# The low halves of three gate slabs on GpSimd instead of VectorE, in a two-layer hybrid decoder trunk

## The reference

```python
proj = jnp.einsum('bsd,dn->bsn', h, w_in)
cq, ckv, kr, qkv_b, qkv_c, iq, ik, iw, gate_logits = split_columns(proj)
# the indexer of C: 16 heads
dots = jnp.einsum('bqhd,bsd->bqhs', iqi, ik)
score = jnp.einsum('bqhs,bqh->bqs', jax.nn.relu(dots), iwi) * idx_scale
# the gates: 3 x 1024 columns of w_in
g_a, g_b, g_c = jnp.split(jax.nn.sigmoid(gate_logits), 3, axis=-1)
merged = g_a * y_a + g_b * y_b + g_c * y_c
x = x + g1 * (merged @ w_out)
```

## Time and profile before

| | us |
|---|---|
| median of 3 runs | 975.89 |
| the runs | 975.89, 978.88, 974.9 |
| the profiled execution's own time | 971.84 |
| its span, first to last instruction | 969.6 |
| TensorE busy | 913.4 |
| VectorE busy | 708.9 |
| ScalarE busy | 499.6 |
| GpSimd busy | 29.4 |

### The profile page before, as it was taken

One profiled execution on the slowest core, in us unless ns is written; L12 is line 12 of the kernel. 1 busy time (PEld: TensorE's weight loads), 2 busy tenths in 40 slices (PEclk: granted clock), 3 DMA queues, 4 the chain that ended last, 5 costly groups with the idle time before them and its releaser, 6 DMA issues.

```text
span 969.6 us, 12842 instructions
## 1 busy us (share of the span) xinstructions
PE 913.4 (94%) x5020; PEld 779.2 (80%) x5020; DVE 708.9 (73%) x1145; ACT 499.6 (52%) x738; POOL 29.4 (3%) x53
## 2 busy tenths in 40 slices
PE   8998979998997999999989998899989889999998
PEld 5887969976975788888868997898679668888886
DVE  5987889787787667585675788988878856565454
ACT  6455775455447343443573478374453754343441
POOL 1010000000000000000010000000000000000000
PEclk9999999999999999999999999999999999999999
DMA  9978723414652757775466884251445345645441
GB/s 377 410 305 365 249 88 131 174 44 174 261 204 100 272 208 272 285 280 202 150 241 210 303 320 155 88 205 56 173 170 223 138 150 196 244 152 205 173 174 44
DMA packets 29581, 198.12 MB, mean 204 GB/s; under 512 B 3281, under 2 KB 3793, under 8 KB 7506
## 3 DMA queue, kind: packets, MB, share of 16 engines
q1 hardware_dynamic: 23474, 155.22, 42.8%
q0 software_dynamic: 5760, 41.95, 11.5%
q10 hardware_dynamic: 288, 0.14, 0.1%
HBM read 196.24 MB, written 1.05 MB: 203 GB/s over the span
## 4 chain that ended last, share of the span: by engine, by line
PE 55%; DVE 28%; ACT 8%; issue 5%; DMA 3%; DVEq 0%; ACTq 0%
PE bank L566 13%; PE bank L567 13%; PE bank L568 13%; DVE w_lo L1315 9%; PE bank L527 3%; PE bank L529 3%; PE bank L528 3%; ACT w_hi L965 3%; DMA raw<-in_slabs_dram 3%; DVE front L1322 3%; DVE acc L1622 2%; DVE score L1531 2%; DVE score L1549 1%; PE bank L902 1%; DVE acc L1322 1%
## 5 line engine op out<-in xcount | busy, mean ns | idle before, releaser
L1315 DVE TENSOR_TENSOR w_lo<-raw,w_hi 128x2048 fp32r<-128x2048 f32 (+2 forms) x146 | 316.3, 2172 | 111.2 <-ACT w_hi L965 109.2
L965 ACT ACTIVATE w_hi<-raw 128x2048 fp32r<-128x2048 f32 (+2 forms) x146 | 262.8, 1806 | 96.5 <-PE bank L568 65.1
L566 PE MATMUL bank<-w_hi,h_hi 128*128 128x512 f32 x536 | 214.1, 400 | 10.4 <-DVE w_lo L1315 7.3
L567 PE MATMUL bank<-w_hi,h_lo 128*128 128x512 f32 x536 | 210.6, 393 | 0.0
L568 PE MATMUL bank<-w_lo,h_hi 128*128 128x512 f32 x536 | 210.4, 393 | 0.0
L566 PEld LDWEIGHTS bank<-w_hi,h_hi 128*128 128x128 f32 x536 | 101.5, 189 | 36.1 <-issue 7.9
L568 PEld LDWEIGHTS bank<-w_lo,h_hi 128*128 128x128 f32 x536 | 101.5, 189 | 22.1
L567 PEld LDWEIGHTS bank<-w_hi,h_lo 128*128 128x128 f32 x536 | 101.4, 189 | 19.9
L527 PE MATMUL bank<-h_hi,w_hi 128*128 128x256 f32 x384 | 111.5, 290 | 5.7 <-DVE w_lo L1315 5.7
L528 PE MATMUL bank<-h_lo,w_hi 128*128 128x256 f32 x384 | 108.6, 283 | 0.0
L529 PE MATMUL bank<-h_hi,w_lo 128*128 128x256 f32 x384 | 108.6, 283 | 0.0
(11 more groups left out here) (206 smaller groups left out, 1399.9 us busy)
## 6 DMA issues: line engine op xcount, KB each, us to landing
raw<-in_slabs_dram SPq DMA_DIRECT2D x124, 1024.0 KB, 4.8
front<-in_ada_dram POOLq DMA_DIRECT2D x31, 1024.0 KB, 5.7
acc<-in_ada_dram POOLq DMA_DIRECT2D x9, 1024.0 KB, 8.1
raw<-in_slabs_dram SPq DMA_DIRECT2D x16, 552.0 KB, 5.0
front<-in_ada_dram SPq DMA_DIRECT2D x5, 1024.0 KB, 10.7
raw<-in_slabs_dram SPq DMA_DIRECT2D x6, 768.0 KB, 5.9
proj<-in_ada_dram SPq DMA_DIRECT2D x2, 1024.0 KB, 8.6
x_t<-in_x_dram SPq DMA_DIRECT2D x2, 512.0 KB, 4.4
```

Of the source, the lines that this page charges most:

```text
L566: nc.tensor.matmul(o, hh, wh, start=first, stop=False)
L567: nc.tensor.matmul(o, hl, wh, start=False, stop=False)
L965: nc.scalar.activation(w_hi[:, n % RING, 0:w], raw[:, n % RING, 0:w], ACT.Copy).then_inc(hi_ready.sem, 1)
L1315: nc.vector.tensor_tensor(w_lo[:, n % RING, 0:w], raw[:, n % RING, 0:w], w_hi[:, n % RING, 0:w], ALU.subtract).then_inc(lo_ready.sem, 1)
```

## The change

GpSimd makes the low halves of the slabs `S_GATE1`, `S_GATE1 + 1` and `S_GATE1 + 2` in both layers, behind its ten loads and before `spread_gate`, and counts them on a semaphore of its own, `lo_pool`. VectorE no longer makes them. Whoever waits for a low half (SyncE before it reloads a place, TensorE before it multiplies) asks `split(l, s)`, which gives the semaphore and the count for this slab.

```diff
+POOL_LO = [S_GATE1 + g for g in range(3)]
@@
-        lo_ready = event("lo_ready", NS)
+        lo_ready = event("lo_ready", NS - len(POOL_LO))
+        lo_pool = event("lo_pool", len(POOL_LO))
@@
+        def split(l, s):
+
+            if s in POOL_LO:
+                return lo_pool.sem, lo_pool.at(l, POOL_LO.index(s) + 1)
+            return lo_ready.sem, lo_ready.at(l, s + 1 - sum(p < s for p in POOL_LO))
@@ SyncE, load
                 if n >= RING:
-                    sp.wait_ge(lo_ready.sem, n - RING + 1)
+                    sp.wait_ge(*split(*divmod(n - RING, NS)))
@@ GpSimd
                 for _ in range(10):
                     load_ada(n)
                     n += 1
+                for s in POOL_LO:
+                    m = l * NS + s
+                    pool.wait_ge(hi_ready.sem, m + 1)
+                    nc.gpsimd.tensor_tensor(w_lo[:, m % RING, :], raw[:, m % RING, :], w_hi[:, m % RING, :], ALU.subtract)\
+                        .then_inc(lo_pool.sem, 1)
 
                 pool.wait_ge(idx_sc.sem, idx_sc.at(l, IDX_HEADS))
@@ TensorE
             def slab(l, s):
-                pe.wait_ge(lo_ready.sem, lo_ready.at(l, s + 1))
+                pe.wait_ge(*split(l, s))
@@ VectorE, in the loop over the indexer's heads
                     if h == 7:
                         pair_norm(1, C_B, ss16b, 2 * A_QK, K_FAC)
-                        lo(l, S_GATE1)
-                    if h == 11:
-                        lo(l, S_GATE1 + 1)
@@ VectorE, after it
                 k_rows(0)
                 k_rows(1)
-                lo(l, S_GATE1 + 2)
```

## The result

The changed kernel takes 980.09 us (median of 17 runs), the kernel before 973.63 us over as many: 1.0061 times as long, 95% interval 1.0047 to 1.0075, so 4.6 to 7.3 us more (the two medians alone lie 6.5 us apart). Forecast were 6.4 us more and 982.3 us. The 2.2 us between the forecast time and the measured one come from the starting value: three runs had given 975.89.

A forecast was written before the change was run, and what follows sets the result against it. TensorE, busy 94% of the span, was taken to set the pace, so only its waits count. Layer 0's +3.4 us and layer 1's +3.05 sum to +6.4; 975.89 + 6.4 = 982.3 us, range 972.5 to 988.

The forecast's parts named there:

- the chain's VectorE rows: Around the indexer, read alone they make the change worth 3 x 2.2 us in each of two layers, 13.3 us.
- Rival A: GpSimd's subtraction is short (near 2.1 us) or VectorE isn't held: -3.3 us, 972.6 us; chance 0.20.
- GpSimd's time: Duration p of each moved subtraction on GpSimd, taken as 4.2 us; break-even at 2.7 us.
- the doubled copy rate: Two operands read one after the other at the 128x1024 copy's 1.044 us: 2 x 2 x 1.044 = 4.2 us.
- The hold: While GpSimd reads SBUF, VectorE instructions with two SBUF operands stand still, up to 4.2 us per subtraction.
- near 5: Expected sign: TensorE's wait before the pair transposes (L745, starting at 147.0 us) is near 5 us.
- 137.9 + 2p: End of heads 8 to 11 on VectorE in layer 0, for a subtraction of p us; 146.3 us forecast.
- the 0.35 taken off: Layer 1's wait at L745 is already 0.35 us longer, so +3.05 us there against +3.4 in layer 0.
- The fourth slab: TensorE waits for VectorE's low half of the fourth gate slab, 2.9 to 3.9 us late: +3.4 us in layer 0.
- nothing for the clock: A fallen clock behind TensorE's idle 142 to 147 us adds at most some 0.8 us a layer; not counted.
- The reload of the ring: SyncE's reloads wait for GpSimd's subtractions; costs nothing while low halves come earlier than TensorE asks.
- the late gate row: GpSimd's gate row copy queues behind the third subtraction; its reader starts at 251.7 us, so lateness costs nothing.

The follow-up runs named there:

- e1: The changed kernel with GpSimd's three subtractions narrowed from 2048 to 64 words a partition; 0.9956 of the kernel before, 4.3 us below it.
- e2: The changed kernel with each GpSimd subtraction replaced by three memsets, about 4.7 us together, that read nothing; 0.995 of the kernel before, 4.9 us below it.
- e12: The changed kernel with 24 matmuls that nobody reads in front of TensorE's wait for the last relu; 1.0064 of the kernel before.
- e7: The kernel before with only the third low half moved to GpSimd, VectorE making the first two; 1.0074 of the kernel before.
- e11: The kernel of e7 with 24 matmuls that nobody reads in front of TensorE's wait for the fourth gate slab; 1.0032 of the kernel before.
- e6: The kernel before with only the second low half moved to GpSimd, VectorE making the first and third; 1.0076 of the kernel before.

## Why the prediction was right

- **What bounds the kernel.** That TensorE's waits and not the chain's VectorE rows measure what there is to gain stands: all but freed of the three subtractions, the kernel gained 4.3 to 4.9 us (e1, e2) and not 13.3. Rival A's -3.3 us lies within both intervals.
- **GpSimd's time.** 4.6 us when not held, against 4.2 from the doubled copy rate: this term was 0.4 us short. The Trainium skill's 4497 ns (GPSIMD Engine Reference, section "Performance versus the Vector engine") is the nearer one.
- **The hold.** Right in mechanism and in place. Counted from the kv slab's low half (1.57 us off the trace), head 8 was forecast at 142.9 and came at 142.8; head 11 ended at 146.1 (146.3); the third subtraction ran from 148.5 to 153.1 (148.8 to 153.0); L1565's sum began at 158.0 (157.4 to 158.4). L745 started at 146.7 (147.0), but with a wait of 4.0 us and not near 5: TensorE had already waited 0.9 us instead of 0.3 for a relu in front of head 8. The first two subtractions ended 0.2 and 0.3 us later than forecast (129.3 and 135.1).
- **What was luck in the size.** With 4.6 us in place of 4.2 the prediction's own formula, 137.9 + 2p, gives 147.1 us for the end of head 11, 1.0 us later than measured, and the same steps make each layer 1.2 us longer and the sum 8.8 us, above the measured interval. The short term was taken up by others: the first subtraction began 1.1 us before the forecast 124.9, still beside VectorE's own, and a head takes 0.80 to 0.83 us, not the 0.85 to which it was rounded. Layer 1 has a small misreading: its wait at L745 is longer by 0.26 us; 0.33 is by how much its transposes start later than 474.3 us behind those of layer 0, and only that supports the 0.35 taken off.
- **What is held.** I had put the hold down to VectorE instructions with two SBUF operands. The first head's TENSOR_SCALAR reads one tensor and a scalar column and was held for 3.2 us all the same, so the condition as worded was too narrow; the Trainium skill (SBUF — State Buffer, section "Who interferes with whom") names `tensor_scalar`, which can run in a 2-port mode, beside instructions with two SBUF inputs. This row agrees that it is held; in which mode it ran, no row shows.
- **The fourth slab.** Here a step was wrong and did little harm. I let TensorE wait there for VectorE and counted nothing for the clock. In the trace TensorE comes 0.24 us later than the low half, at 168.98 us (167.4 less the offset), held back by the half clock behind its 4.0 us wait. The two run side by side and are about equal (e12), which the prediction had worked out for the range but not as the state that would hold.
- **Where no VectorE lateness covers it, the same omission was a miss.** It made e7's expectation 1.004 where 1.0074 was measured, and e11, back at 1.0032 with the full clock, shows that the clock was most or all of the difference.
- **The reload of the ring and the late gate row** cost nothing, as said: no wait for either is among TensorE's.

## What to carry to other kernels

As these runs show it, work moved from VectorE to GpSimd is beside VectorE's only as long as GpSimd doesn't read SBUF or VectorE runs nothing that it holds: price such a move on VectorE, at up to GpSimd's duration minus VectorE's. Before moving work off an engine, list the waits of the engine that sets the pace, since the chain of waits shows the engine's whole row and not what is behind it; in this kernel the order of the same work gave 11 to 12 us, and the second step of it came from reading which wait the first had made. Where a change makes an idle stretch of TensorE longer, keep the granted clock behind it as a term of its own: here it stayed full behind 2.0 us, was half behind 2.8 and 4.0, and either behind 3.2.

## What the runs showed of the hardware

- The hold goes both ways. GpSimd's first subtraction lasts 5.51 us instead of 4.6 while VectorE's own one is running, and in e6 the gate row's copy, 1.04 us elsewhere, takes 2.28 beside VectorE's subtraction:

```profile
141.64 2.28 POOL L479 COPY ikz<-mod 128x1024 f32<-128x1024 f32 x1 [6.87 <-PE bank L752]
```

- The clock isn't settled by the length of the idle stretch alone: in front of the gate slab at 93.2 to 93.5 us TensorE is idle for 3.23 us in both traces of the unchanged kernel, and the granted clock of the stretch behind it is 1.00 in one and 0.50 in the other. This alone moves executions of one kernel by more than a microsecond.
